# Head steps ahead of the row's own work in the delta stage, and a shorter chain from the norms' sums to their broadcast root

## The reference, cut to what matters

```python
def rmsnorm(x, g):
    xf = x * lax.rsqrt(jnp.mean(x * x, axis=-1, keepdims=True) + EPS)
    return xf * g
def l2norm(t):
    return t * lax.rsqrt(jnp.sum(t * t, axis=-1, keepdims=True) + EPS)
```

## Time and profile before

| | before |
|---|---|
| median of 3 runs | 3462.91 us (3462.80 to 3464.23) |
| the profiled execution | 3464.78 us, span 3463.0 us |
| mean granted TensorE clock | 0.967 |
| busy | PE 3294.6 us (95%), DVE 2049.1, ACT 1328.1, POOL 528.5 |
| chain that ended last | PE 84%, DVE 9%, ACT 3%, POOL 2% |

### The profile page before, as it was taken

The page is one execution under the profiler, slowest core; times in us unless marked ns, Lnnn a source line. Parts: engine busy times, 40 slices in busy tenths (PEclk is TensorE's granted clock), DMA queues, the critical chain, the costliest instruction groups (busy, mean ns, idle before and its releaser), DMA issues.

```text
span 3463.0 us, 41094 instructions
## 1 busy us (share of the span) xinstructions
PE 3294.6 (95%) x16321; PEld 2722.7 (79%) x16321; DVE 2049.1 (59%) x3543; ACT 1328.1 (38%) x2338; POOL 528.5 (15%) x547
## 2 busy tenths in 40 slices
PE   8999999999999999999899997899898999999998
PEld 5764889998888888888788875778686667778887
DVE  5765987776888888887555435445443345443332
ACT  3131238883444444444322224444443124232221
POOL 0001009971222222221000000000000000000000
PEclk9999999999999999999899998999899999999999
DMA  6426234569999999996355422121121122222222
GB/s 253 138 70 221 74 123 173 191 218 345 335 329 333 338 330 327 338 327 250 105 187 183 144 70 91 58 86 67 64 83 55 41 82 79 90 79 96 96 94 75
DMA packets 190207, 574.42 MB, mean 166 GB/s; under 512 B 16576, under 2 KB 82112, under 8 KB 171712
## 3 DMA queue, kind: packets, MB, share of 16 engines
q1 hardware_dynamic: 152144, 367.96, 30.4%
q0 software_dynamic: 37872, 203.84, 16.0%
HBM read 523.89 MB, written 47.84 MB: 165 GB/s over the span
## 4 chain that ended last, share of the span: by engine, by line
PE 84%; DVE 9%; ACT 3%; POOL 2%; DMA 1%; issue 1%; SPq 0%; DVEq 0%; ACTq 0%; POOLq 0%
PE ps L231 11%; PE ps L232 10%; PE ps L233 10%; PE ps L1602 5%; PE ps L1603 5%; PE ps L1601 5%; PE ps L1362 4%; PE ps L1364 4%; PE ps L1363 4%; PE ps L240 4%; PE ps L581 2%; PE ps L316 2%; PE ps L171 1%; DVE Wl L223 1%; PE ps L584 1%; POOL peerg_OH L1354 1%
## 5 line engine op out<-in xcount | busy, mean ns | idle before, releaser
L223 DVE TENSOR_TENSOR Wl<-W,Wh 128x1024 fp32r<-128x1024 f32 x363 | 438.6, 1209 | 706.5 <-ACT Wh L217 700.3
L217 ACT ACTIVATE Wh<-W 128x1024 fp32r<-128x1024 f32 x363 | 377.6, 1041 | 567.2 <-PE ps L233 532.1
L1362 PE MATMUL ps<-peer_Hh,Wh 128*128 128x384 f32 x1024 | 349.5, 341 | 8.9 <-DVE Wl L223 8.9
L1364 PE MATMUL ps<-peer_Hh,Wl 128*128 128x384 f32 x1024 | 346.3, 338 | 0.0
L1363 PE MATMUL ps<-peer_Hl,Wh 128*128 128x384 f32 x1024 | 346.0, 338 | 0.0
L1570 POOL DMA_INDIRECT peerv_UV<-peer_uv,peer_EX x128 | 209.8, 1639 | 641.1 <-DVE peer_Y L1638 583.5
L1601 PE MATMUL ps<-peerv_VH,peer_HTh 128*128 128x512 f32 x768 | 299.0, 389 | 2.2 <-DVE peer_HTl L1664 2.2
L1603 PE MATMUL ps<-peerv_VH,peer_HTl 128*128 128x512 f32 x768 | 300.5, 391 | 0.0
L1602 PE MATMUL ps<-peerv_VL,peer_HTh 128*128 128x512 f32 x768 | 300.3, 391 | 0.0
L231 PE MATMUL ps<-f_Hh,Wh 128*128 128x512 f32 x672 | 262.3, 390 | 2.2 <-DVE Wl L223 2.2
L233 PE MATMUL ps<-f_Hh,Wl 128*128 128x512 f32 x672 | 261.5, 389 | 0.0
(11 more groups left out here) (497 smaller groups left out, 6499.3 us busy)
## 6 DMA issues: line engine op xcount, KB each, us to landing
W<-peer_u SPq DMA_DIRECT2D x128, 512.0 KB, 8.0
peerv_VR<-peer_v SPq DMA_DIRECT2D x128, 512.0 KB
gates_dram<-peerg_GB SPq DMA_DIRECT2D x12, 2048.0 KB, 7.3
peerv_GR<-gates_dram SPq DMA_DIRECT2D x32, 768.0 KB, 8.6
f_AW<-w_ada POOLq DMA_DIRECT2D x48, 512.0 KB, 4.2
W<-w_gate SPq DMA_DIRECT2D x44, 512.0 KB, 3.2
W<-w_up SPq DMA_DIRECT2D x44, 512.0 KB, 3.2
swa_AW<-w_ada POOLq DMA_DIRECT2D x32, 512.0 KB, 4.5
```

The lines of the kernel that those rows point to most:

```text
L217: A.then_inc(e.activation(w_parts(i)[0], w_raw(i), ACT.Copy), ("w_hi", i))
L223: V.then_inc(e.tensor_tensor(lo, w_raw(i), hi.bitcast(F32), SUB), ("w", i))
L1362: e.matmul(o, hi[:, k, :], H2[0][:, k, 0:TD], start=k == 0, stop=False)
L1364: ins = e.matmul(o, lo[:, k, :], H2[0][:, k, 0:TD], start=False, stop=k == 7)
```

## The change

Three edits. (1) The generators of the rows are advanced twice per step: the first half (splits, norms, PE's whole part) stays ahead of the heads, the second half (convolution, silu, square, eviction) comes behind them. The last part of the stage (`keys_*`) gets its yields doubled. (2) In `Norm` the sums of the 8 tiles accumulate on 4 columns, the two DVE operations are dropped, ACT reads the bank and takes the root with scale and bias, and diagonal and broadcast are done in four pieces of 128 columns. (3) In the rows' L2 norms ACT reads the bank with a bias of EPS in place of DVE's addition.

```diff
+    eps1 = tiny(1)
         def sq_pe(self, e, k):
             A.wait_ge(e, (self.tag, "sq", k))
             for tb, sl in enumerate(sl4):
-                ins = e.matmul(self.bank[:, 8 * tb + k:8 * tb + k + 1], self.square(k)[:, sl], ones[:, 0:1],
-                               start=True, stop=True)
+                ins = e.matmul(self.bank[:, tb:tb + 1], self.square(k)[:, sl], ones[:, 0:1], start=k == tb == 0,
+                               stop=k == 7, skip_group_check=True)
-        def mean_dve(self, e):
-            PE.wait_ge(e, (self.tag, "sq", 7))
-            V.then_inc(e.tensor_reduce(self.s, self.bank[:, 0:32].rearrange("p (b k) -> p b k", b=4), AX.X, ADD))
-            V.wait_ge(e, V.n)
-            V.then_inc(e.tensor_scalar(self.s, self.s, 1.0 / D, EPS, MUL, ADD), (self.tag, "mean"))
         def root_act(self, e):
-            V.wait_ge(e, (self.tag, "mean"))
-            A.then_inc(e.activation(self.s, self.s, ACT.Sqrt), (self.tag, "root"))
+            V.wait_ge(e, "eps")
+            PE.wait_ge(e, (self.tag, "sq", 7))
+            A.then_inc(e.activation(self.s, self.bank[:, 0:4], ACT.Sqrt, bias=eps1, scale=1.0 / D), (self.tag, "root"))
         def root_dve(self, e):
             ...
-            V.then_inc(e.tensor_tensor(v4(self.square(8)), bc4(ident), self.s.unsqueeze(2).broadcast_to([128, 4, 128]),
-                                       MUL), (self.tag, "diag"))
+            for tb, sl in enumerate(sl4):
+                V.then_inc(e.tensor_scalar(self.square(8)[:, sl], ident, self.s[:, tb:tb + 1], None, MUL),
+                           (self.tag, "diag", tb))
         def root_pe(self, e):
-            V.wait_ge(e, (self.tag, "diag"))
-            PE.then_inc(e.matmul(self.bank, ones, self.square(8), start=True, stop=True), (self.tag, "rstd"))
+            for tb, sl in enumerate(sl4):
+                V.wait_ge(e, (self.tag, "diag", tb))
+                PE.then_inc(e.matmul(self.bank[:, sl], ones, self.square(8)[:, sl], start=True, stop=True),
+                            (self.tag, "rstd"))
     def ada1_dve(e):
+        V.then_inc(e.memset(eps1, EPS), "eps")
     def row_steps(rows, make_head):
             live = [g for g in live if next(g, "end") != "end"]
+            if rows:
+                next(rows)
     def rows_pe(e):
             ...
             yield
+            yield
     def rows_act(e):
             if n - 1 in norm_of:
-                V.wait_ge(e, ("nr1", m))
-                A.then_inc(e.activation(r, r, ACT.Sqrt), ("nr2", m))
+                if m >= 3:
+                    V.wait_ge(e, ("ndg", m - 3))
+                PE.wait_ge(e, ("nsum", m))
+                A.then_inc(e.activation(r, ps(6 + m % 2)[:, 0:4], ACT.Sqrt, bias=eps1), ("nr2", m))
+            yield
             if n < NROW:
                 kind, h, c = ROWS[n]
     def rows_dve(e):
                 r = R4[:, 4 * d:4 * d + 4]
-                PE.wait_ge(e, ("nsum", m))
-                V.then_inc(e.tensor_scalar(r, ps(6 + m % 2)[:, 0:4], 1.0, EPS, MUL, ADD), ("nr1", m))
                 A.wait_ge(e, ("nr2", m))
+            yield
             if n < NROW and ROWS[n][0] == "qkv":
```

More of the change, by code:

```diff
@@ L315, in sq_pe, with root_act @@
             for tb, sl in enumerate(sl4):
-                ins = e.matmul(self.bank[:, 8 * tb + k:8 * tb + k + 1], self.square(k)[:, sl], ones[:, 0:1],
-                               start=True, stop=True)
+                ins = e.matmul(self.bank[:, tb:tb + 1], self.square(k)[:, sl], ones[:, 0:1], start=k == tb == 0,
+                               stop=k == 7, skip_group_check=True)
             PE.then_inc(ins, (self.tag, "sq", k))
-        def mean_dve(self, e):
+        def root_act(self, e):
+            V.wait_ge(e, "eps")
             PE.wait_ge(e, (self.tag, "sq", 7))
-            V.then_inc(e.tensor_reduce(self.s, self.bank[:, 0:32].rearrange("p (b k) -> p b k", b=4), AX.X, ADD))
-            V.wait_ge(e, V.n)
-            V.then_inc(e.tensor_scalar(self.s, self.s, 1.0 / D, EPS, MUL, ADD), (self.tag, "mean"))
-        def root_act(self, e):
-            V.wait_ge(e, (self.tag, "mean"))
-            A.then_inc(e.activation(self.s, self.s, ACT.Sqrt), (self.tag, "root"))
+            A.then_inc(e.activation(self.s, self.bank[:, 0:4], ACT.Sqrt, bias=eps1, scale=1.0 / D), (self.tag, "root"))
         def root_dve(self, e):
@@ L361, in dve @@
         def dve(self, e):
-            self.norm.mean_dve(e)
             self.norm.root_dve(e)
@@ L519, in ada1_dve @@
         shift_dve(e, (1,))
-        n1.mean_dve(e)
         shift_dve(e, (2,))
@@ L1697, in fin_dve @@
         ff1.scales(e)
-        nf.mean_dve(e)
         nf.root_dve(e)
@@ L2177, in keys_act @@
             yield
+            yield
     def keys_dve(e):
-        yield
-        yield
+        for _ in range(4):
+            yield
         PE.wait_ge(e, ("nbc", 15))
         lat_norm_dve(e, "k", 2, 6)
+        for _ in range(4):
+            yield
+        lat_scale_dve(e, "k", KL, 2, "g_kv_lat_2", 7)
         yield
-        yield
-        lat_scale_dve(e, "k", KL, 2, "g_kv_lat_2", 7)
         yield
@@ L2927, in end_dve @@
     def end_dve(e):
-        ne.mean_dve(e)
         ne.root_dve(e)
```

## The result

| | before | after | predicted |
|---|---|---|---|
| median, us | 3462.86 | 3438.51 | 3434.6 |
| lowest to highest of 4 runs | 3456.24 to 3464.23 | 3431.21 to 3439.59 | 3425 to 3448 |
| after / before | | 0.9931 [0.9914, 0.9948] | 0.992 |
| profiled execution, us | 3464.8 | 3439.59 | 3436.5 |
| its span, us | 3463.0 | 3437.8 | |

The changed kernel is faster by 0.7%. It gains 24.4 us between the medians and 25.2 us between the two spans, where 28.3 were forecast.

What follows compares the result with a forecast made beforehand. PE was taken as the bound, busy 3294.6 of 3463.0 us. Terms of 23.0 (rows' order), 4.8 (six norms) and 0.5 (n1) sum to 28.3 us: profiled 3464.8 becomes 3436.5, median 3434.6, range 3425 to 3448.

Steps and rivals of the forecast that it cites:

- Part 1: Delta stage: moving the rows' second half (convolution, silu, square, eviction) behind the heads gains 23.0 us in all.
- 22, 38, 54: waits for k: Even heads' s3: k's eviction no longer stands behind the row's on ACT; three waits of 1.72 us go, 5.2 us.
- 23, 39, 55: new wait on L223: The row's eviction, now behind the next head's s0 on ACT, makes PE wait 0.6 us per step, 1.8 us lost.
- rows 23, 39, 55: clock: With the waits ahead of them gone, these rows return from 7.4, 8.4 and 8.1 to 5.7 us, gaining 6.8 us.
- 5 and 40: Heads 0 and 5, s2: the convolution no longer stands ahead of DVE's subtraction and matrix; 6.2 us gained.
- the case that was worked out with it, 3440.6 us: A drain of about 1380 ns on each table load lengthens waits in the delta stage, some 6 us less gain; chance 0.04.
- None waits by this sum: About 13 qkv steps with two heads alive: the later square still precedes PE's sum by 0.5 us, so PE never waits.
- the last sentence of the forecast: Sign of error: PE waits for L2087 or L223 in many steps, L316's spacing grows, or low clock moves to other rows.
- The case with 5 us more from rows 6, 26, 41 and 42: Rival: these slow rows of the delta stage recover their clock too, giving 3429.6 us; chance 0.14.
- Part 2: Norms: dropped DVE operations and a broadcast in pieces gain 0.8 us in each of six norms, 4.8 us.
- DVE drops two operations there: Seventh norm, n1, beside a chain of DVE multiplies that DMA feeds: two fewer DVE operations gain 0.5 us.
- a slower accumulation on the same columns: Norms: summing on 4 columns leaves the 256 matmuls as they are, gain nothing; any delay would show in their spacing.

Runs made afterwards that it cites:

- the change's second trace: Profile from a repeat of the unaltered changed kernel, on the same chip as its parts: 3435.58 us, ratio 0.9918 to the kernel before.
- The filler: Kernel before, plus eight unread small matmuls on PE ahead of its wait for k's eviction in steps 22, 38 and 54: 3456.84 us, ratio 0.9982.
- The kernel with the wait moved: Changed kernel with ACT's wait for the EPS column moved ahead of its squares in n1: 3436.3 us, ratio 0.9919 to the kernel before.
- the norms alone: Kernel before with only both kinds of norms changed, the rows' order as before: 3457.45 us, ratio 0.9985.
- the order alone: Kernel before with only the rows' second half moved behind the heads, all norms as before: 3441.07 us, ratio 0.9931.
- the kernel with one added operation: Changed kernel with one more DVE operation (0.75 us) in the convolution of 18 qkv rows from row 11 on: 3447.3 us, ratio 0.9954.

## Why the prediction held, step by step

**Part 1** was forecast at 23.0 us. The two stage windows give 23.2, the kernel with this part alone 22.4, the change's second trace 25.6. By its own steps, from the gap between the last matmul of a row and the first of the next, and from the rows' own lengths:

| step | predicted gain | measured gain |
|---|---|---|
| 22, 38, 54: waits for k | 5.2 | 7.3 (1.9 + 2.5 + 2.8) |
| 23, 39, 55: new wait on L223 | -1.8 | -2.6 |
| rows 23, 39, 55: clock | 6.8 | 6.6 |
| 25 | 3.4 | 3.8 |
| 5 and 40 | 6.2 | 6.3 |
| 41 | 3.2 | 3.7 |
| 4 and 26: not foreseen | 0 | -1.6 |
| rows 6, 7, 9, 26, 41, 42: clock | 0 | -0.5 |
| sum | 23.0 | 23.0 |

The mechanism of every term was right, but that the sum came out to a tenth is luck: misses of up to 2.1 us on one side and 1.6 on the other cancel. The rest up to 23.2 us lies in rows and steps that the table leaves out: steps 2 and 12 lose 0.5 us each, rows 2, 3 and 5 gain 1.1.

In steps 22, 38 and 54 the gaps gave more than the waits, 7.3 us against 5.2. The filler, which removes no wait for k, gives back 0.6 and 0.8 us in the gaps of steps 38 and 54 all the same, so 1.4 us of the rest are clock in the small matmuls between the rows. The other 0.2 us in each step is what a wait costs beyond its listed length: listed idle time begins at a matmul's end, and without a wait the next starts ahead of that (a row's matmuls are 0.39 us long and start 0.23 apart). So the new waits on L223, 0.61 us each, cost 0.85 each, 2.6 in place of the 1.8 forecast. The ends of the remaining waits, in PE's timeline of after: step 4's sum, step 25, a new wait on L223 (step 39), step 40 and step 41.

```profile
2132.22 1.46 PE L2062 MATMUL ps<-consts_sb,gdnc_AN 128*128 128x1 f32 x8 [1.56 <-ACT gdnc_AN L2092]
...
2338.20 0.66 PE L171 MATMUL ps<-consts_sb,gdnh_c 128*128 128x128 f32 x4 [1.77 <-ACT gdnc_KD L2292]
...
2453.72 0.47 PE L231 MATMUL ps<-mix2h_Hh,Wh 128*128 128x512 f32 x1 [0.61 <-DVE Wl L223]
2463.77 1.12 PE L171 MATMUL ps<-consts_sb,gdnc_KD 128*128 128x128 f32 x4 [2.53 <-DVE gdnh_c L2332]
2479.91 0.66 PE L171 MATMUL ps<-consts_sb,gdnh_c 128*128 128x128 f32 x4 [2.30 <-ACT gdnc_KD L2292]
```

1.8, 0.6 and 2.5 us were forecast for steps 25, 39 and 40; they are 1.77, 0.61 and 2.53. The 0.6 was in part luck. The forecast's working has tile 40 ready at 2464.6 and PE there at 2464.3, which is 0.3, and takes 0.6 without a term for the rest; in the trace the tile is ready 8.9 us after row 39 starts (8.6 by the working) and PE has finished at 8.4 (8.3). Against the waits of the earlier trace rows that is the plain rule that a wait falls by the length of what stood ahead of its releaser, until something else is later. The work that was then late next was named correctly: the chain exponentials, table load, eviction, L217, L223. Its load brought no drain: in step 38 of after the load runs from 2449.48 to 2450.76 us and the eviction starts at 2450.78; in n1 the load's row ends at 27.74 and the root starts at 27.76. The Trainium skill ("ScalarE: Activation LUTs", What ACT_TABLE_LOAD costs) adds a drain of about 1380 ns to each load; this trace does not show it, and the case that was worked out with it, 3440.6 us, rested on waits of 2.0 us in steps 23, 39 and 55 that are not there.

What I missed in part 1 is step 4. There silu and square now stand behind a head's exponentials on ACT, with no slack in front of the square's sum, and PE waits 1.56 us. The wait of 2.53 us ahead of row 5 is gone in return, but the small matmuls ran slower, and the gap grew by 1.1 (by 0.4 in the second trace). Short waits of 0.23 and 0.25 us in steps 12 and 26 are of the same kind. "None waits by this sum" was thus wrong for these two; step 4, with one head alive, was left out of it. In steps like 29 the estimated slack of 0.5 us was right: in seven of them the square ends 0.49 to 0.61 us ahead of PE's sum. In step 27 it is only 0.18.

**The rows' clock.** The filler shows the premise, that the waits of 1.72 us lower the clock. The clock was moved as well as mended, as the last sentence of the forecast feared, but in balance. Row 26 recovered (6.66 to 5.72 us) and row 7 went from 8.62 to 7.40, while rows 6, 9, 41 and 42 became slower by 0.25 to 0.9 us each. The windows over rows 6, 41 and 26 of after:

```profile
2151.30:2159.50 8.20, 8.20 (x27) 6.51 (x26) 3.31 (x4) 1.58 (x2) 0.00 (x0) 0.68 0.19 64
...
2467.20:2474.50 7.30, 7.30 (x27) 5.93 (x26) 3.33 (x4) 3.49 (x4) 0.00 (x0) 0.77 0.05 15
...
2338.60:2344.30 5.70, 5.70 (x27) 4.42 (x25) 4.20 (x6) 1.62 (x5) 0.00 (x0) 1.00 0.00 0
```

The forecast left rows 7 and 9 out of its list of slow rows. The case with 5 us more from rows 6, 26, 41 and 42 did not come: only row 26 recovered, behind a wait that is still 1.77 us long, and the other three, which still follow a wait or a slow row, cost 1.7 us more than before.

**Part 2** was forecast at 0.8 us a norm. From the start of the last sum to the first scaled tile the six norms behind n1 take 25.0 us before and 20.2 after, so 4.7 us were gained of the forecast 4.8; in the change's second trace it is 4.1. The two differ by 0.6 in m2, whose broadcast (2.1 us before) ran faster in the first. f2 gained 0.69 (4.19 to 3.50), 0.63 of it in the chain shown above (3.74 to 3.11). There the reduction and the scaling fall away (0.43 as forecast). The root starts to the diagonal's start in 0.58 us in place of 0.45: -0.13, forecast -0.1. PE starts 0.34 us after the diagonal does, in place of 0.75: 0.41, forecast 0.46, because a piece takes 0.28 us and not 0.23. The broadcast to the scaling takes 0.08 more. Ahead of it, ACT starts 0.03 us behind the last sum's end where DVE started 0.11 behind. So the piece was mis-sized by 0.05, and two terms of 0.08, one each way, were missing.

**n1** was forecast at +0.5 us and came out at -0.4 (36.3 in place of 35.9 us for its first scaled tile; 0.2 of that had arisen by PE's last sum). The step that failed is "DVE drops two operations there": it looked at DVE alone, while ACT's table load, 1.28 us, slipped behind the wait for PE. The kernel with the wait moved shows it. From the last sum on it gains 0.5 us on before (10.13 to 9.65), just what was forecast, and the load had cost 0.6.

**The largest part of the missing 3.1 us** lies in the final norm of the first block, nf. PE's 64 small sums there took 8.56 us before and 11.25 in the profiled execution of after:

```profile
1649.28 8.56 PE L316 MATMUL ps<-consts_sb,DG 128*128 128x1 f32 x64
```

```profile
1648.79 11.25 PE L317 MATMUL ps<-consts_sb,DG 128*128 128x1 f32 x64
```

That would have been the sign of a slower accumulation on the same columns. It is not that: the change again took 8.98 us for the same 64 and the kernel with the moved wait 8.81, though the norms alone took 11.66; and of the kernels with the old 32 columns, which accumulate nothing, the order alone took 8.71 and the filler 11.11:

```profile
1646.30 11.11 PE L316 MATMUL ps<-consts_sb,DG 128*128 128x1 f32 x64
```

The granted clock in that stretch was 0.83 before and 0.62 after. Why it differs from one execution to the next stays open. With 2.7 us here, 0.9 in n1 and 0.1 in the other norms, 3.7 us are accounted for against 3.1 missing; part 1 gave 0.2 more than forecast, and 0.4 was not followed. The change's second measurement, 27.9 us between the medians, is within half a microsecond of the forecast's 28.3. The range's ends don't follow from its own terms: 3429.6 less 3 is 3426.6, and 3441.4 with 6 and 2.8 is 3450.2, where it says 3425 and 3448. The measured 3438.51 lies inside either.

## What to carry to other kernels

When an engine that evicts or transforms for PE holds work of its own that nobody waits for yet, put that work behind what PE waits for; the gain is the length of what stood ahead, until the next-latest releaser. Count a wait of PE twice, once as idle time and once in the clock of the matmuls behind it, for here 16 us of idle time brought 7.5 us of clock with it, though not every wait does. And before adding to an engine's work in such an order, read how much earlier than PE it is in each repetition of the step: it was 0.5 us in most steps here, and 2.3 us more in each turned a gain of 28 us into a loss of 9.

## What the runs showed of the hardware

- Idle stretches of only 1.72 us on PE left the next 5.7 us row at 0.67 to 0.77 of the clock; eight small matmuls put into each brought it to 1.00 and the kernel 6 us down. The length of the wait alone doesn't decide: 1.77 us in step 9 (before and after) and in step 25 (after) left the next row at 1.00, as did 0.61 us in steps 23, 39 and 55, while 1.00 us in step 29 of the kernel with one added operation left it at 0.85. There 4.6 us more idle time went with 6.2 us more busy time in the stage.
- In n1 an activation table load that is tied to an instruction with two waits ran behind the wait for PE (26.46 us), with one wait ahead of it (21.65 us). Loads of 1.28 us were followed by their instruction within 0.02 us (step 38: 2450.76 and 2450.78).
- The same 64 sums of nf took 8.6 to 9.4 us in some executions and 11.1 to 11.7 in others, with either layout of the sums; the granted clock was 0.83 in one and 0.62 in another.
- Eight records of 128 columns cost PE 2.08 us at the low clock, two of 512 columns 2.07, so cutting a broadcast in four costs PE nothing. On DVE four pieces took 0.87 us, the whole 0.69.
